# Weighing and summing the adaLN blocks of the conv-FFNs on GpSimd and VectorE instead of TensorE

## What is computed

```python
c_act = jax.nn.silu(c)                      
for l in range(DEPTH):                      
    mod = c_act @ ada_w[l] + ada_b[l]       
    sh1, sc1, gt1, sh2, sc2, gt2 = jnp.split(mod, 6, axis=-1)
```

```python
hcv = causal_dwconv(u @ w_up, conv_w, conv_b)     
g, v = hcv[..., :D_FF], hcv[..., D_FF:]
return (gelu(g) * v) @ w_down
```

## Time and profile before

| | |
|---|---|
| three runs | 1850.48, 1851.52, 1865.01 us |
| span of the profiled execution, first to last instruction | 1848.6 us |
| the profiled execution's own time | given as this span alone; the median lies 2.9 us above it |
| TensorE busy | 1789.5 us (97%) |
| VectorE busy | 1291.4 us (70%) |
| ScalarE busy | 1014.5 us (55%) |
| GpSimd busy | 29.5 us (2%) |
| granted TensorE clock, mean | 0.992 |

### The profile page before, as it was taken

How to read it: one execution, slowest core, us unless ns; L and a number is a source line. 1 busy time by engine, 2 the same in 40 slices (tenths; PEclk the granted TensorE clock), 3 DMA queues, 4 the chain that set the end, 5 groups by cost and what they waited for, 6 DMA issues and landing times. The chain is left out here.

```text
span 1848.6 us, 37836 instructions
## 1 busy us (share of the span) xinstructions
PE 1789.5 (97%) x15229; PEld 1660.0 (90%) x15229; DVE 1291.4 (70%) x1997; ACT 1014.5 (55%) x1582; POOL 29.5 (2%) x48
## 2 busy tenths in 40 slices
PE   7999999999999899999999999999998999999999
PEld 7996788889889698998989999989998999998999
DVE  6848777676777987777777767665556875676555
ACT  6645565555576765555556654454445565455443
POOL 0000000000000000000000001000000000100000
PEclk9999999999999999999999999999999999999999
DMA  8540566766775566566634430445553442044553
GB/s 325 182 159 1 195 227 242 269 254 257 263 278 181 218 236 241 216 217 253 249 112 174 144 115 3 161 159 185 202 183 133 140 160 92 12 173 160 184 203 114
DMA packets 44897, 336.17 MB, mean 182 GB/s; under 512 B 4976, under 2 KB 5232, under 8 KB 6768
## 3 DMA queue, kind: packets, MB, share of 16 engines
q1 hardware_dynamic: 38736, 277.89, 41.5%
q0 software_dynamic: 4608, 50.33, 7.2%
q10 hardware_dynamic: 1440, 6.33, 0.9%
HBM read 333.48 MB, written 1.05 MB: 181 GB/s over the span
## 5 line engine op out<-in xcount | busy, mean ns | idle before, releaser
L686 DVE TENSOR_TENSOR w_lo<-raw,w_hi 128x1024 fp32r<-128x1024 f32 x526 | 639.3, 1224 | 379.5 <-ACT w_hi L677 369.5
L677 ACT ACTIVATE w_hi<-raw 128x1024 fp32r<-128x1024 f32 x526 | 555.0, 1060 | 589.9 <-PE unit L708 375.6
L706 PE MATMUL unit<-h_hi,w_hi 128*128 128x256 f32 x2656 | 751.0, 283 | 23.6 <-DVE h_lo L2124 8.0
L707 PE MATMUL unit<-h_lo,w_hi 128*128 128x256 f32 x2656 | 742.7, 280 | 0.0
L708 PE MATMUL unit<-h_hi,w_lo 128*128 128x256 f32 x2656 | 742.4, 280 | 0.0
L706 PEld LDWEIGHTS unit<-h_hi,w_hi 128*128 128x128 f32 x2656 | 503.3, 190 | 35.4 <-issue 22.6
L708 PEld LDWEIGHTS unit<-h_hi,w_lo 128*128 128x128 f32 x2656 | 505.4, 190 | 0.0
L707 PEld LDWEIGHTS unit<-h_lo,w_hi 128*128 128x128 f32 x2656 | 503.2, 189 | 1.3
L706 PE MATMUL acc<-mv_hi,w_hi 128*128 128x256 f32 x640 | 177.1, 277 | 0.0
L707 PE MATMUL acc<-mv_lo,w_hi 128*128 128x256 f32 x640 | 177.1, 277 | 0.0
L708 PE MATMUL acc<-mv_hi,w_lo 128*128 128x256 f32 x640 | 177.1, 277 | 0.0
(11 more groups left out here) (415 smaller groups left out, 1982.9 us busy)
## 6 DMA issues: line engine op xcount, KB each, us to landing
raw<-w_in SPq DMA_DIRECT2D x263, 1024.0 KB, 4.8
ada_ring<-ada_in POOLq DMA_DIRECT2D x32, 1536.0 KB, 7.6
h<-rows_in ACTq DMA_DIRECT2D x5, 512.0 KB, 4.8
keep<-gates_in ACTq DMA_DIRECT2D x1, 1280.0 KB, 10.1
par<-par_in ACTq DMA_DIRECT2D x1, 1036.0 KB, 10.9
x<-x_in SPq DMA_DIRECT2D x2, 512.0 KB, 4.9
out<-x SPq DMA_DIRECT2D x4, 256.0 KB, 2.3
con<-con_in ACTq DMA_DIRECT2D x1, 950.0 KB, 18.0
```

The source lines that it names most:

```text
L677: act(half(w_hi, c, k), raw[c % RAW][:, CW // 2 * k:CW // 2 * (k + 1)], ACT.Copy).then_inc(S("high_parts"), 1)
L686: tt(half(w_lo, c, k), raw[c % RAW][:, CW // 2 * k:CW // 2 * (k + 1)], half(w_hi, c, k).bitcast(f32), ALU.subtract).then_inc(S("chunk_spli ...
L706: mm(out, w, m, start=first, stop=False)
L707: mm(out, w, ml, start=False, stop=False)
```

## The change

GpSimd takes the weighing and the sum over the 8 row tiles for the 22 blocks (`weigh`): two products in place over 128 x 4 x 384 with `cact` broadcast, then three additions that halve the tiles (4 x 384, 2 x 384 and 384 elements). VectorE turns the squares of the remaining 128 x 384 tile and sums each over its 32 columns (`dve_ada_summed`), where it copied one column before. TensorE loses these blocks and its waits for them. A slot is free for the next load when VectorE has turned its block (`ada_turned`), no longer when TensorE has read it. Four semaphores of the SSD stage (`dt_log`, `dt_decays`, `c_act`) become one (`dt_act_steps`), with the same order of steps; GpSimd waits for its third step before the first block.

```diff
 pe_ffn:
-            if l == 1:
-                pe_ada(pe, 22, misc[0])
...
-                    if l == 0:
-                        pe_ada(pe, 2 + k, misc[k], i)
-                    elif k == 0:
-                        pe_ada(pe, 23, misc[1], i, 1)
...
-                if l == 0:
-                    pe.wait_ge(S("ada_turned"), p - 1)
-                    pe_ada(pe, p, misc[p % 2])
-                elif p == 14:
-                    pe.wait_ge(S("ada_turned"), 29)
-                    pe_ada(pe, 29, misc[1])
...
-            pe.wait_ge(S("ada_turned"), 16 if l == 0 else 30)
 dve_ffn (at the same places; blocks 22, 23 and 29 likewise):
-                    dve_ada(dve, p, misc[p % 2], i)
+                    dve_ada_summed(dve, p, i)
 GpSimd:
+        POOL_BLOCKS = list(range(2, 16)) + list(range(22, 30))
+            def load(n):
                 s = SLOT[n]
                 if TURN[n] > 1:
                     before = max(m for m in range(n) if SLOT[m] == s)
-                    pool.wait_ge(S("ada_rows"), before + 1)
+                    if before in SUMMED:
+                        pool.wait_ge(S("ada_turned"), before + 1)
+                    else:
+                        pool.wait_ge(S("ada_rows"), ROWS_AT[before])
                 ada_load(pool, s, n)
+            def weigh(n):
+                tiles = ada_slot[SLOT[n]]
+                pool.wait_ge(S(f"ada_loaded{SLOT[n]}"), 16 * TURN[n])
+                for a in (0, 4):
+                    by = cact[:, a:a + 4].unsqueeze(2).to_broadcast([P, 4, ADA_W])
+                    ins = nc.gpsimd.tensor_tensor(tiles[:, a:a + 4, :], tiles[:, a:a + 4, :], by, ALU.mult)
+                link(ins)
+                for k in (4, 2):
+                    link(nc.gpsimd.tensor_tensor(tiles[:, 0:k, :], tiles[:, 0:k, :], tiles[:, k:2 * k, :], ALU.add))
+                nc.gpsimd.tensor_tensor(tiles[:, 0, :], tiles[:, 0, :], tiles[:, 1, :], ALU.add
+                                        ).then_inc(S("ada_summed"), 1)
+            load(0)
+            load(1)
+            pool.wait_ge(S("dt_act_steps"), 3)
+            for n in range(1, 2 * ADA_N):
+                both = n + 1 < 2 * ADA_N and SLOT[n + 1] != SLOT[n]
+                if both:
+                    load(n + 1)
+                if n in SUMMED:
+                    weigh(n)
+                if not both and n + 1 < 2 * ADA_N:
+                    load(n + 1)
 VectorE:
+        def dve_ada_summed(dve, n, i=None, per=2):
+            dve.wait_ge(S("ada_summed"), at(i, per, SUMMED[n]))
...
+            nc.vector.transpose(ada_turned[:, :], ada_slot[SLOT[n]][:, 0, :]).then_inc(S("ada_turned"), 1)
+            dve.wait_ge(S("ada_turned"), at(i, per, n + 1))
...
+            nc.vector.tensor_reduce(dst, ada_turned[:, :].rearrange("p (a b) -> p a b", b=32), AX.X, ALU.add
+                                    ).then_inc(S("ada_cols"), 1)
```

More of the change, by code:

```diff
@@ L1152, in dve_ssd @@
                 if n == 1:
-                    dve.wait_ge(S("dt_decays"), 2)
+                    dve.wait_ge(S("dt_act_steps"), 4)
                     for p in (32, 96):
@@ L1407, in pair @@
                 if l == 0 and p >= 2:
-                    dve_ada(dve, p, misc[p % 2], i)
+                    dve_ada_summed(dve, p, i)
                 elif l == 1 and p == 1:
-                    dve_ada(dve, 22, misc[0])
+                    dve_ada_summed(dve, 22)
                 elif l == 1 and p == 2:
-                    dve_ada(dve, 23, misc[1], i, 1)
+                    dve_ada_summed(dve, 23, i, 1)
             pair(0)
@@ L1430, in dve_ffn @@
                 if l == 0:
-                    dve_ada(dve, p, misc[p % 2])
+                    dve_ada_summed(dve, p)
                 elif p == 14:
-                    dve_ada(dve, 29, misc[1])
+                    dve_ada_summed(dve, 29)
             ahead(dve_split, dve, c0 + 45)
@@ L1690, in build, with pool_ada @@
         TURN = [SLOT[:n].count(SLOT[n]) + 1 for n in range(2 * ADA_N)]
-        def pool_ada(pool):
-            for n in range(2 * ADA_N):
+        POOL_BLOCKS = list(range(2, 16)) + list(range(22, 30))
+        PE_BLOCKS = [n for n in range(2 * ADA_N) if n not in POOL_BLOCKS]
+        SUMMED = {n: j + 1 for j, n in enumerate(POOL_BLOCKS)}
+        ROWS_AT = {n: j + 1 for j, n in enumerate(PE_BLOCKS)}
+        def pool_ada(pool, link):
+            def load(n):
                 s = SLOT[n]
@@ L1697, in pool_ada, with pe_ada @@
                     before = max(m for m in range(n) if SLOT[m] == s)
-                    pool.wait_ge(S("ada_rows"), before + 1)
+                    if before in SUMMED:
+                        pool.wait_ge(S("ada_turned"), before + 1)
+                    else:
+                        pool.wait_ge(S("ada_rows"), ROWS_AT[before])
                 ada_load(pool, s, n)
-        def pe_ada(pe, n, bank, i=None, per=2):
+            def weigh(n):
[20 more added lines that the diff above has]
+                    load(n + 1)
+        def pe_ada(pe, n, bank):
             s = SLOT[n]
-            pe.wait_ge(S(f"ada_loaded{s}"), at(i, 16, 16 * TURN[n]))
-            if i is not None:
-                pe.wait_ge(S("ada_turned"), at(i, per, n - per + 1))
+            pe.wait_ge(S(f"ada_loaded{s}"), 16 * TURN[n])
             for k in range(8):
@@ L1712, in pe_ada, with dve_ada @@
             ins.then_inc(S("ada_rows"), 1)
-        def dve_ada(dve, n, bank, i=None, per=2):
+        def dve_ada(dve, n, bank):
             w = ADA_W // 32
-            dve.wait_ge(S("ada_rows"), at(i, per, n + 1))
+            dve.wait_ge(S("ada_rows"), ROWS_AT[n])
+            if n >= 1:
+                dve.wait_ge(S("ada_cols"), n)
+            nc.vector.transpose(ada_turned[:, :], bank[:, 0:ADA_W]).then_inc(S("ada_turned"), 1)
+            dve.wait_ge(S("ada_turned"), n + 1)
+            nc.vector.tensor_copy(ada_cols[:, w * n:w * (n + 1)],
+                                  ada_turned[:, :].rearrange("p (a b) -> p a b", b=32)[:, :, 0]
+                                  ).then_inc(S("ada_cols"), 1)
+        def dve_ada_summed(dve, n, i=None, per=2):
+            w = ADA_W // 32
+            dve.wait_ge(S("ada_summed"), at(i, per, SUMMED[n]))
             if i is not None or n >= 1:
                 dve.wait_ge(S("ada_cols"), at(i, per, n))
-            nc.vector.transpose(ada_turned[:, :], bank[:, 0:ADA_W]).then_inc(S("ada_turned"), 1)
+            nc.vector.transpose(ada_turned[:, :], ada_slot[SLOT[n]][:, 0, :]).then_inc(S("ada_turned"), 1)
             dve.wait_ge(S("ada_turned"), at(i, per, n + 1))
             dst = ada_cols[:, w * n:w * (n + 1)] if i is None else ada_cols[:, bass.ds(i * (per * w) + w * n, w)]
-            nc.vector.tensor_copy(dst, ada_turned[:, :].rearrange("p (a b) -> p a b", b=32)[:, :, 0]
-                                  ).then_inc(S("ada_cols"), 1)
+            nc.vector.tensor_reduce(dst, ada_turned[:, :].rearrange("p (a b) -> p a b", b=32), AX.X, ALU.add
+                                    ).then_inc(S("ada_cols"), 1)
         GAP = {"ffn0": 0, "lru": 16, "ffn1": 20, "in2": 30}
@@ L1732, in pe_gap @@
             if n == 0:
-                pe.wait_ge(S("c_act"), 1)
+                pe.wait_ge(S("dt_act_steps"), 3)
             x_updated(pe, stage)(0)
@@ L2932, in _ @@
             pool.wait_ge(loaded[0], 16)
-            pool_ada(pool)
+            pool_ada(pool, Chain(pool, S("pool_link")))
             for l in range(2):
```

12 lines of the change are left out of this document (6 added, 6 removed).

## The result

The changed kernel takes 1975.6 us, the median of 4 runs (1972.1 to 1980.9), against 1851.0 before: ratio 1.066, 95% interval 1.063 to 1.070. It is 125 us slower. The forecast had the sign and the mechanism, and half of the size: +58 us predicted, and the time lies above the range. The profiled execution took 1978.5 us, with a span of 1976.7.

A forecast was written before the change was run, and what follows sets the result against it. TensorE was taken to set the pace in the conv-FFNs; with exclusion, -1.6 (block 2) + 55 (twelve pairs) + 5 (block 15) + 0 (FFN 1) = +58 us, so 1909 us, range 1812 to 1942.

The forecast's parts named there:

- TensorE loses 36 us: TensorE in both conv-FFNs: 22 blocks of 1.63 us each no longer run there, 36 us less work.
- The reduction, the later slot, the merged semaphore: VectorE's sum adds 0.4 us a pair, hidden by idle time; gap loads come later with time to spare; merged semaphore 0.
- GpSimd needs 11.7 us a block: GpSimd's weighing: 5760 elements per partition at 2.03 ns, 11.7 us a block, kept at 9 to 13.
- Exclusion: VectorE's two-SBUF-input instructions and GpSimd's SBUF-reading ones wait for each other; likeliest case, chance 0.50, range 1880 to 1945 us.
- Half of what could be packed: 22.8 us: FFN 0 pair under exclusion: middle of 20.7 (best packed) and 24.9 us (nothing packed); twelve pairs +55 us.
- Only block 15 has a short pair, +5: End of FFN 0: block 15's pair has two chunks, is 8 us late, some caught up during `w_down`: +5 us.
- Block 2, put at -1.6: Start of FFN 0: block 2 is weighed during pairs 0 and 1, costs nothing and wins 1.6 us.
- FFN 1 unchanged: Second conv-FFN: a turn of two pairs and one block takes 34.8 us against 34.85 now, so 0.
- The clock, nothing added: TensorE idles some 20% in FFN 0, but its granted clock is 1.00 in the stretches, so nothing is added.
- no interference: Rival: GpSimd and VectorE do not hold each other up; pair 16.61 us, time 1815.5 us, chance 0.31.
- GpSimd alone pays: Rival: VectorE's instructions go first and GpSimd yields; 20.7 us a pair, +17 us, time 1869, chance 0.13.
- GpSimd too slow by itself: Rival: without interference, GpSimd's long products or chain waits set the pace from 16.6 us a block; 1860 to 1905, chance 0.06.

## Why the prediction was off

- *TensorE loses 36 us*: right. The run without arithmetic took 35 us less than before, each run once.
- *The reduction, the later slot, the merged semaphore (three became one) cost nothing*: right within 1 or 2 us, by the same run. The reduction took 0.553 us, 0.55 predicted.
- *GpSimd needs 11.7 us a block, from 2.03 ns an element*: about right. The two products took 5.46 us (6.2 by my rate) and two sums and the last 5.44 + 1.00 us undisturbed: 11.9. That the load is hidden because it is issued one block ahead is right for FFN 0; in FFN 1 blocks 23 to 29 share a slot, and GpSimd waits some 8 to 10 us for each to land, in time that nobody needs.
- *Exclusion, chosen for two lengthened rows*: right, on thin evidence (0.02 to 0.03 us longer for 0.16 us of overlap). What is shown now: VectorE's instructions with two SBUF inputs and GpSimd's instructions that read SBUF hold each other up, and it goes by instruction. Beside GpSimd's two-input instructions VectorE waits as well; beside its one-input products nearly all the waiting is GpSimd's (1.24 us by themselves, up to 3.4 beside VectorE). The Trainium skill (SBUF — State Buffer, "Who interferes with whom") says that a VectorE instruction with two SBUF inputs contends with any GpSimd instruction that reads SBUF, and not with one that only writes it. The runs with one-input products and the write-only run agree. That the later one waits until the other is done, as the prediction put it, does not hold for one-input products: the `w_lo` that began 0.69 us after one took 1.23 us. There the measurement decides.
- *"Half of what could be packed: 22.8 us" a pair*: this is the step that failed. The pair took 25.08 us, just above my bound with nothing packed, 24.9. That the two are so close is in part luck: VectorE was held off for 10.1 us a pair and not for 11.7, and besides its own 13.1 us it was idle for 1.9, which the bound did not have. I argued from a share of VectorE's one-input work, as if GpSimd's burst fell at a random place. It does not: the burst starts with VectorE's own turn, and the next instructions in VectorE's order are two `w_lo` and `mv_lo`, all with two inputs. The taps come at 363.22 us, when the burst, prolonged by the wait on both sides, has 0.9 us left. The order that I had written down in the prediction's own GpSimd paragraph ("behind its wait stand the two halves of the split, then `mv_lo` and the taps") would have given it. Twelve pairs at the measured 6.84 us would be 82 instead of 55.
- *Only block 15 has a short pair, +5*: mis-sized. Pair 14 is short too: the turns 13 to 15 lay 26.2 us apart and lie 42.9 apart now, +17. Block 2, put at -1.6, came at +6: its weighing fell beside the first pairs and held VectorE off there too, and the first turn came that much later.
- *FFN 1 unchanged, "34.8 against 34.85"*: wrong by 23 us in all, 37.09 us a turn. I compared VectorE's sum over a turn with TensorE's. The sum was about right: VectorE is held off for 8.3 us a turn (busy 167.20 us in five turns, 125.46 without the arithmetic), where I had 9.6. But it comes in one lump, and TensorE, which had no idle time before, then waits (12 us for `mv_lo` in this stage) and does not make it up. Small pieces took this away: 33.3 us a turn.
- *The clock, nothing added*: 0.9 us a pair, about 10 us in the eleven pairs, by the run that kept TensorE busy. The earlier trace rows showed it only where TensorE has no idle time, which says nothing about 26% of it.
- The rivals: no interference is refuted. That GpSimd alone pays is refuted for the changed kernel, whose `w_lo` take up to 6.77 us, and is nearly what happens with one-input products. GpSimd too slow by itself is refuted: a block took it 11.9 us undisturbed, as said above, far from the 16.6 from which this rival decides.

## What to carry to other kernels

An idle engine is not free when its instructions and those of the engine that feeds the bottleneck hold each other up: list the instructions of both with inputs in SBUF, and, as a first estimate, add the times of VectorE's two-input ones and GpSimd's instead of overlaying them. Where the burst falls decides as much as how long it is: look at the instructions that stand directly behind the one that releases it, and cut the burst into small pieces. Here that took 81 us off, and still left the kernel 43 us slower than before. Here the same work went to ScalarE (products) and VectorE (halving sums, the first of them between two halves of a split) and made the kernel 1.2% faster than the one before, where GpSimd made it 6.6% slower.

## What the runs showed of the hardware

- GpSimd's product with a per-partition scalar took 1.24 us for 384 elements where VectorE did not hold it up, against 0.82 us for the product of two tensors of that size. Beside VectorE's two-input instructions the first grew to as much as 3.4 us and the second to 1.9.
- Its product of two tensors of 1536 elements took 2.74 us, 1.8 ns an element; memsets of 1536 elements took 1.4 us and held nothing up.
- VectorE's reduction of 128 x 3072 with the summed elements 384 apart took 5.79 us; three halving sums over the same data 0.95, 0.96 and 0.96 us for 768 elements and 0.56 for the last 384, 3.4 in all.
- With 6.4 us of idle time of TensorE in each pair its granted clock was 0.86 in FFN 0, and matmuls in those stretches on unused data brought it back to 0.99.
